# Where the last unit's activation split stands at the end of an expert

## The reference

```
for e in range(8):                      # top 2 of 8 experts, D_FF_EXPERT = 3584
    g, u = split(t @ w_gu[e])           # t: 256 x 1024, w_gu[e]: 1024 x 7168
    out += gates[:, e] * ((silu(g) * u) @ w_down[e])     # w_down[e]: 3584 x 1024
```

## Time and profile before

| | |
|---|---|
| median of 3 runs | 1511.94 us (1511.2 to 1513.96) |
| the profiled execution, its own time | 1520.08 us |
| its span, first to last instruction | 1517.9 us |
| mean granted TensorE clock | 0.992 |
| busy: TensorE, VectorE, ScalarE | 1466.1, 1167.1, 971.9 us |

### The profile page before, as it was taken

How to read it: one execution, slowest core, us unless ns; L and a number is a source line. 1 busy time by engine, 2 the same in 40 slices (tenths; PEclk the granted TensorE clock), 3 DMA queues, 4 the chain that set the end, 5 groups by cost and what they waited for, 6 DMA issues and landing times.

```text
span 1517.9 us, 20148 instructions
## 1 busy us (share of the span) xinstructions
PE 1466.1 (97%) x8256; PEld 1233.0 (81%) x8256; DVE 1167.1 (77%) x1129; ACT 971.9 (64%) x979; POOL 38.6 (3%) x41
## 2 busy tenths in 40 slices
PE   5989999999999999999999999999999999999987
PEld 2868899998977878888888888888878888888865
DVE  2546654444897779889879889988888997988977
ACT  1445543432557587777777777777777778776763
POOL 0110000000000100000000000000000000000000
PEclk9999999999999999999999999999999999999999
DMA  9576676655843569999989999989999998999983
GB/s 376 212 275 244 230 269 226 225 192 189 283 160 123 218 227 374 375 384 372 381 342 373 369 380 392 376 334 391 374 372 370 368 378 357 376 372 393 384 341 137
DMA packets 102528, 474.83 MB, mean 313 GB/s; under 512 B 8316, under 2 KB 39180, under 8 KB 53280
## 3 DMA queue, kind: packets, MB, share of 16 engines
q1 hardware_dynamic: 99408, 464.81, 81.2%
q0 software_dynamic: 2160, 6.92, 1.2%
q10 hardware_dynamic: 864, 1.76, 0.3%
HBM read 468.65 MB, written 4.81 MB: 312 GB/s over the span
## 4 chain that ended last, share of the span: by engine, by line
PE 74%; issue 12%; DMA 6%; DVE 5%; ACT 3%; POOL 0%; POOLq 0%; SPq 0%; ACTq 0%; DVEq 0%
PE bank L1626 15%; PE bank L1628 15%; PE bank L1627 15%; PE bank L1632 6%; PE bank L1634 5%; PE bank L1633 5%; DMA raw<-ada_w 2%; PE bank L1643 2%; PE bank L1974 1%; DMA raw<-moe 1%; PE bank L1928 1%; PE bank L1929 1%; PE bank L1930 1%; PE bank L2135 1%; DVE hid L1322 1%
## 5 line engine op out<-in xcount | busy, mean ns | idle before, releaser
L1493 DVE TENSOR_TENSOR low<-raw,high 128x2048 fp32r<-128x2048 f32 x333 | 753.2, 2289 | 106.2 <-ACT high L833 104.0
L833 ACT ACTIVATE high<-raw 128x2048 fp32r<-128x2048 f32 x333 | 634.4, 1921 | 145.8 <-DMA raw<-moe 143.9
L1626 PE MATMUL bank<-high,hidH 128*128 128x512 f32 x896 | 350.4, 391 | 5.3 <-DVE low L1493 5.3
L1628 PE MATMUL bank<-high,hidL 128*128 128x512 f32 x896 | 349.8, 390 | 0.0
L1627 PE MATMUL bank<-low,hidH 128*128 128x512 f32 x896 | 349.4, 390 | 0.0
L1632 PE MATMUL bank<-hidH,high 128*128 128x256 f32 x736 | 210.9, 287 | 3.6 <-DVE hidL L977 2.9
L1633 PE MATMUL bank<-hidL,high 128*128 128x256 f32 x736 | 208.1, 283 | 0.0
L1634 PE MATMUL bank<-hidH,low 128*128 128x256 f32 x736 | 208.1, 283 | 0.0
L1626 PEld LDWEIGHTS bank<-high,hidH 128*128 128x128 f32 x896 | 168.7, 188 | 40.6 <-DVE low L1493 5.7
L1628 PEld LDWEIGHTS bank<-high,hidL 128*128 128x128 f32 x896 | 168.6, 188 | 35.2
L1627 PEld LDWEIGHTS bank<-low,hidH 128*128 128x128 f32 x896 | 168.7, 188 | 34.8
(11 more groups left out here) (237 smaller groups left out, 1247.4 us busy)
## 6 DMA issues: line engine op xcount, KB each, us to landing
raw<-moe SPq DMA_DIRECT2D x336, 1024.0 KB, 6.4
raw<-ada_w SPq DMA_DIRECT2D x48, 1024.0 KB, 7.1
raw<-ffn_gu SPq DMA_DIRECT2D x44, 512.0 KB, 5.1
raw<-ffn_down SPq DMA_DIRECT2D x11, 1024.0 KB, 7.0
raw<-w_in SPq DMA_DIRECT2D x8, 1024.0 KB, 11.9
raw<-conv_pw SPq DMA_DIRECT2D x16, 512.0 KB, 5.7
raw<-w_o SPq DMA_DIRECT2D x4, 1024.0 KB, 7.4
raw<-conv_pw SPq DMA_DIRECT2D x4, 1024.0 KB, 5.6
```

The source lines that it names most:

```text
L833: a.activation(high[:, m % SPLITS, :], raw[:, n % RAWS, :], ACT.Copy).then_inc(S("high_ready"), 1)
L1493: v.tensor_tensor(low[:, n % RAWS, :], raw[:, n % RAWS, :], high[:, m % SPLITS, :].bitcast(F32), ALU.subtract).then_inc(S("low_ready"), 1)
L1626: pe.matmul(out, xh, wh, start=start, stop=False)
L1628: return pe.matmul(out, xl, wh, start=False, stop=stop)
```

## The change

For all experts but the last, the split of the last unit's transposed activations goes one place forward, past the split of piece 43, on ScalarE and on VectorE alike. TensorE's list and the queue of the loads are as before.

```
@@ ScalarE, body(e, last)
+                    act_high(e, UNITS_E - 1)
                     parts(e, ahead(UNITS_E - 1), PER_E + 2, last)
-                    act_high(e, UNITS_E - 1)
                     if not last and passes:
                         gather_out(e + 1)
                     if not last and not passes and e % 2:
@@ VectorE, body(e, last)
+                    act_low(e, UNITS_E - 1)
                     parts(e, ahead(UNITS_E - 1), PER_E + 2, last)
-                    act_low(e, UNITS_E - 1)
                     parts(e, PER_E + 2, PER_E + LEAD - 1, last)
```

## The result

The changed kernel is slower: 1518.66 us median against 1513.96 us for the kernel before, 11 runs each; the ratio is 1.0028, with a 95% interval of 1.0015 to 1.0040, so +4.2 us with 2.3 to 6.1 (the medians themselves are 4.7 us apart). With more runs the kernel before itself stands 2.0 us above the median that the prediction was made on (1511.94 of three). The forecast was +2.3 us and a range that ended at 1516.3; direction and mechanism were as forecast, the size was not.

The account below looks back on a forecast made before the run. TensorE, busy 97% of the span, was taken as the bound. Odd ends +3.2 us, less 0.65 for even ends and 0.25 given back, made +2.3 on 1511.94: 1514.2 us, range 1511.4 to 1516.3.

Parts of the forecast that it names:

- direction and mechanism: Slower, because piece 43 on ScalarE delays the gather copies that TensorE's low groups need after experts 1, 3 and 5.
- The bound and the place: TensorE sets the end; of seven expert ends, the three odd ones with a gather lose time.
- The three waits: TensorE idles before the first tokL group after experts 1, 3 and 5, 0.98 to 1.13 us each.
- a term of 3.2: Loss at the odd ends: 3 x 1.06 = +3.2 us, bounds 2.9 to 4.2.
- the discount in the sum: Taken off the odd ends' +3.2 us: 0.65 for even ends and 0.25 for shorter later waits, leaving +2.3.
- The 0.65: Half of the 1.3 us saved at expert 4's end, since timed runs need not have its late transfer.
- the gain at the even ends: Expert 4's wait for upL goes, -1.3 us; bounds 0 to 5.3 us over four even ends.
- The 0.25: TensorE's odd pauses let the loads catch up, shortening later eact waits by 0.25 of 1.9 us.
- The slip of ScalarE's list: Piece 43 about 2.9 us later, pieces behind it at most 1.9 us later; cost to TensorE zero.
- cover named for pieces 43 to 47: Slack before TensorE wants the delayed pieces: 3.3 us for piece 43, 5 us for piece 44 after odd experts.
- the loads are the true pace: Rival: loads set the pace, so odd waits do not show; 0 to -1.3 us, about 1511.3; chance 0.13.
- The clock rival: Clock falls to 0.50 for 6.8 us after each odd wait, 10.2 us in all, 1524.4; chance 0.04.

Follow-up runs that it names:

- dose: The changed kernel with piece 44 as well as piece 43 on ScalarE between act_high 13 and the gather copies; ratio 1.0091, +13.8 us against the kernel before.
- odd-only: The kernel before with the new order only after experts 1, 3 and 5; ratio 1.0017, +2.6 us.
- the `e_down` experiment: The changed kernel with TensorE doing e_down of unit 12 between the gather's high and low groups; ratio 1.0020, +3.0 us against the kernel before.
- expert 6 alone: The kernel before with the new order after expert 6 only, where no gather follows; ratio 1.0003.
- the experiment that put the copies back: The changed kernel with ScalarE copying expert 6's result out ahead of piece 46; ratio 1.0036, +5.4 us against the kernel before.
- VectorE alone: The kernel before with the new order on VectorE only, ScalarE as before; ratio 0.9998, -0.3 us.

## Why the prediction was right and wrong

**The bound and the place** were right: TensorE alone sets the end, and of the seven places the three with a gather lose. The three waits stand where the prediction put them, ended by what it named, and dose, odd-only and the `e_down` experiment bear it out in their profiles, the first two in their times as well. TensorE's wait was put at 0.98 to 1.13 us and was 1.10; the slower low groups make it 1.17. That is 3.5 us for a term of 3.2, within its bounds of 2.9 to 4.2, and by it the timed change would be +3.5.

**The step that failed is the discount in the sum**, "+3.2 - 0.65 - 0.25". The 0.65 was half of the gain at the even ends. That wait was there in one profile, as the earlier trace rows, and in the profile after it is gone; but it is rare. The profiles with the old order at even ends (before, odd only, the two kernels with later gate steps and otherwise the old order, and three ends of expert 6 alone) hold 19 such ends and this one wait. By that count it is worth 4 x 1.33 / 19 = 0.3 us an execution, an estimate. The timed runs alone can't say whether a gain of 0.65 was there. The 0.25 was what TensorE's pauses would give back, out of 1.9 us of `eact` waits of which 1.35 stand at 558 us, ahead of the first changed place; with a dose of three times 2.74 us the time grew by more than the waits, so no giving back was seen. Without both the sum is 3.5 and the time 1515.4 on the old median.

**The slip of ScalarE's list was costed at nothing**, with cover named for pieces 43 to 47. Those covers held: no profile shows TensorE waiting for one of them. What was left out is the other work on that list, the result copies of expert 6, behind which the fetch, the landings and VectorE's gate steps come later. In profiles it is 0.7 us, and 1.6 us with the gate steps moved. 3.5 and 0.7 add up to the 4.2 measured, but that may be luck, for the 0.7 is not proven by time: the intervals reach 1.4 to 2.1 us on either side, and the experiment that put the copies back did not get faster. It also stays open why the kernels with ScalarE's new order but none of the three waits were at +1.2, +1.5 and, with `e_down` between, +3.0 us (1.4 to 4.7), while VectorE alone was at -0.3. A part of the spread goes with the clock: of 83 timed runs of the kernel before, the 21 with a mean granted clock of up to 0.993 have a median of 1518.3 us, the 19 with 0.996 or more one of 1513.1.

**The range failed for a plainer reason as well**: it was laid around a median of three that further runs moved by 2.0 us. Its upper end, 1516.3, is +4.4 us on the old median and +2.3 on the new. The measured +4.2 would have fallen inside on the old one.

**The rivals.** That the loads are the true pace fell with the dose. The clock rival did not happen at 0.94 us waits: the granted clock was 1.00 around all three, and the row of the 1.16 us wait was a fair guide. The Trainium skill, "TensorE: Matmul & The Clock Gate", "A second HAM failure mode: psum-queue depth-cycling", tells of short idles between matmul groups that made the clock swing; at this size and number this kernel's trace does not show that. With longer waits the clock did fall, as the next section tells.

## What to carry to other kernels

Before an instruction is moved ahead of another on an in-order engine, read what stands behind both: here a 1.9 us split filled a gap for free, and in its new place it stood before copies that the bounding engine wanted 1.2 us after they used to start. A gain that is one late transfer in one profile should be counted at next to nothing until a second profile shows it (here one of 19 places had it), while a loss that the written order makes comes in every execution. The larger find was a wait visible in the same table of waits, 5.3 us in the last expert: moving the work that waits for the fetch two units later made the kernel 0.4% faster (1507.64 us, ratio 0.9961); no version of this study was clearly better.

## What the runs showed of the hardware that was not expected

A short pause of TensorE costs about its length, and some of the longer ones more. The granted clock fell to 0.50 for 3.4 us after all four waits of 2.28 us, after one of three of 2.74 us, and after none of the single waits of 0.94 to 2.02 us; each fall cost about 1.7 us more. Why one pause of 2.74 us had a fall behind it and two had none is open. The one fall of the two-piece kernel, and the window of the wait before it (columns as in the earlier trace rows):

```profile
1013.00:1016.60 3.60, 0.90 (x8) 0.69 (x6) 2.35 (x2) 3.60 (x4) 0.00 (x0) 1.00 0.71 278
1017.70:1021.10 3.40, 3.40 (x15) 3.01 (x14) 1.04 (x1) 3.25 (x6) 0.00 (x0) 0.50 0.01 5
```

Two profiles can also differ by 4.7 us ahead of the place of interest, in code that is the same. Distances between marks of TensorE are steadier: 117.79 us is the undisturbed even distance in every profile but that of the new order on ScalarE alone. They gave the loss at an odd end as 1.17 us three times of three, where some ten timed runs left the whole change uncertain by 1.4 to 2.1 us on either side.
